# A pair of heads' attention scores made side by side on the two halves of TensorE's rows

## What is computed

```
# per block of 128 queries, 8 heads of 64, 2 heads of keys and values, k_top = 256
logits = einsum('bqhd,bsd->bqhs', q_idx, k_idx) * 64 ** -0.5
score = einsum('bqhs,bqh->bqs', relu(logits), w_idx) * 8 ** -0.5
_, sel = top_k(where(causal, score, -inf), k_top)
s = einsum('bqhgd,bqkhd->bqhgk', q, k[sel]) * 64 ** -0.5      # masked where not valid
o = einsum('bqhgk,bqkhd->bqhgd', softmax(s), v[sel])
```

## Time and profile before

| | us |
|---|---|
| median of 3 runs | 3080.78 |
| the three runs | 3079.59 to 3089.05 |
| span of the profiled execution | 3082.3 |
| PE busy in it | 2955.2 |
| DVE busy | 2238.4 |
| ACT busy | 1631.1 |
| selection stage, from the profile | about 2232 to 2897 |

### The profile page before, as it was taken

One profiled execution on the slowest core, in us unless ns is written; L12 is line 12 of the kernel. 1 busy time (PEld: TensorE's weight loads), 2 busy tenths in 40 slices (PEclk: granted clock), 3 DMA queues, 4 the chain that ended last, 5 costly groups with the idle time before them and its releaser, 6 DMA issues. The chain is left out here.

```text
span 3082.3 us, 48442 instructions
## 1 busy us (share of the span) xinstructions
PE 2955.2 (96%) x17512; PEld 2368.1 (77%) x17512; DVE 2238.4 (73%) x3267; ACT 1631.1 (53%) x2923; POOL 297.2 (10%) x683
## 2 busy tenths in 40 slices
PE   6999999999999999999999999999978899999899
PEld 5888888888878886777777888888756667777687
DVE  8888887766576758889879665535278998888553
ACT  5343422232454546777769534222278899988510
POOL 2000000000000001000100000000022333333100
PEclk8999999999999999999999999999978999999999
DMA  4434422257755423111127334232551111111774
GB/s 123 125 106 119 159 73 69 69 184 246 217 172 139 176 99 115 32 29 56 46 68 234 98 118 137 98 124 77 156 117 42 25 37 24 26 39 41 166 223 139
DMA packets 375235, 334.66 MB, mean 109 GB/s; under 512 B 97275, under 2 KB 328187, under 8 KB 368973
## 3 DMA queue, kind: packets, MB, share of 16 engines
q1 hardware_dynamic: 368676, 294.73, 33.4%
q0 software_dynamic: 5600, 36.51, 3.4%
q10 hardware_dynamic: 720, 0.31, 0.0%
HBM read 212.84 MB, written 108.68 MB: 104 GB/s over the span
## 5 line engine op out<-in xcount | busy, mean ns | idle before, releaser
L349 ACT ACTIVATE s_mx_w_hi<-s_mx_raw 128x512 fp32r<-128x512 f32 x224 | 138.5, 628 | 310.1 <-PE p_oa_acc L705 238.2
L705 PE MATMUL p_oa_acc<-s_h_a_hi,s_mx_w_hi 128*128 128x512 f32 x744 | 291.5, 392 | 8.5 <-DVE s_h_a_lo L448 7.1
L705 PE MATMUL p_oa_acc<-s_h_a_lo,s_mx_w_hi 128*128 128x512 f32 x744 | 290.4, 390 | 0.0
L705 PE MATMUL p_oa_acc<-s_h_a_hi,s_mx_w_lo 128*128 128x512 f32 x744 | 290.4, 390 | 0.0
L1821 DVE TENSOR_TENSOR_SCAN s_st_prod<-s_st_soft,s_st_prod 128x512 f32<-128x512 f32 x192 | 234.9, 1269 | 8.3 <-ACT s_st_soft L1748 7.6
L1748 ACT ACTIVATE s_st_soft<-p_st_z 128x512 f32<-128x512 f32 (+3 forms) x320 | 153.4, 533 | 108.5 <-PE p_st_z L1874 107.7
L3565 PE MATMUL p_sa_turn<-s_ident,s_sa_arg 128*128 128x128 f32 x1088 | 164.9, 287 | 42.2 <-ACT s_sa_prob L3163 22.7
L491 DVE TENSOR_TENSOR s_mx_w_lo<-s_mx_raw,s_mx_w_hi 128x512 fp32r<-128x512 f32 x224 | 153.5, 686 | 53.6 <-ACT s_mx_w_hi L349 52.1
L2654 PE MATMUL p_pr_ps<-s_h_hi,s_pr_w_hi 128*128 128x512 f32 (+1 forms) x680 | 183.1, 390 | 1.2 <-DVE s_pr_w_lo L2509 1.0
L2654 PE MATMUL p_pr_ps<-s_h_hi,s_pr_w_lo 128*128 128x512 f32 (+1 forms) x680 | 182.9, 389 | 0.0
L2654 PE MATMUL p_pr_ps<-s_h_lo,s_pr_w_hi 128*128 128x512 f32 (+1 forms) x680 | 182.9, 389 | 0.0
(11 more groups left out here) (465 smaller groups left out, 7366.7 us busy)
## 6 DMA issues: line engine op xcount, KB each, us to landing
s_mx_raw<-in_w_in_a SPq DMA_DIRECT2D x128, 256.0 KB, 3.9
s_pb_ada<-in_w_ada SPq DMA_DIRECT2D x16, 768.0 KB, 6.6
s_pr_raw<-in_w_in SPq DMA_DIRECT2D x21, 512.0 KB, 6.1
s_pr_work<-s_pr_stage SPq DMA_DIRECT2D x38, 256.0 KB, 4.4
d_rot_hi<-s_pr_rot POOLq DMA_DIRECT2D x9, 1024.0 KB, 4.3
d_rot_lo<-s_pr_stage POOLq DMA_DIRECT2D x9, 1024.0 KB, 6.3
d_y_t<-s_mx_y SPq DMA_DIRECT2D x16, 512.0 KB, 5.6
s_oa_y_raw<-d_y_t SPq DMA_DIRECT2D x16, 512.0 KB, 6.7
```

The source lines that it names most:

```text
L705: ins = nc.tensor.matmul(bank, w[:, m, k, :], a[:, m, k, :], start=(k == 0 and n == 0), stop=(k == KH - 1 and n == 2))
```

## The change

Index scores stay as they are (`whole_scores`). Attention scores are made for a pair of heads and one key part at a time. The query tile now has, for each pair, the high part of the even head on partitions 0 to 63 and of the odd head on 64 to 127, and the low parts likewise behind them; this takes four DMAs a block in place of two. A matmul then uses the 64 rows of one head: three products (high·high, high·low, low·high) for each of the two heads, six matmuls in place of four, the two heads' on different rows of the array and into different banks. Both banks must be free before the first of the six. The list of due times alternates the heads within a key part, so that a pair's products stand side by side.

```diff
 def load_queries(sp, to, landed, b, first, rot_hi, rot_lo):
+    if first == ROT_QI:
...
+    pairs = HEADS // 2
+    for part, of in enumerate((rot_hi, rot_lo)):
+        rows = of[first:first + 512, :].rearrange("(c s d) (t n) -> s t d c n", s=2, d=HD, n=P)
+        for side in range(2):
+            sp.dma_start(to[side * HD:side * HD + HD, b % 2, part * pairs:part * pairs + pairs].bitcast(F32), rows[side, ORDER[b]]).then_inc(landed[b % 2], 16)
...
-        ahead = [("attend", qb, 2 * pair + side, m) for side in range(2) for m in range(len(parts(qb)))]
-        timed += [(s - LEAD + (n + 0.5) / len(ahead), p) for n, p in enumerate(ahead)]
+        ahead = [("attend", qb, 2 * pair + side, m) for m in range(len(parts(qb))) for side in range(2)]
+        timed += [(s - LEAD + (n // 2 + 0.5) / (len(ahead) // 2), p) for n, p in enumerate(ahead)]
...
+                    pe.wait_ge(q_in[qb % 2], 64 * (qb // 2 + 1))
...
+            def scores(kind, qb, pair, m):
+                n, width = number[kind, qb, 2 * pair, m], parts(qb)[m][1]
...
+                for side in range(2):
+                    bank_free(n + side)
+                q = (qi_two if kind == "index" else q_two)[:, qb % 2]
+                q_hi, q_lo = q[:, pair], q[:, PAIRS + pair]
+                hi, lo = keys_of(kind, qb, pair, m)
+                for nth, (one, two) in enumerate(((q_hi, hi), (q_hi, lo), (q_lo, hi))):
+                    for side in range(2):
+                        rows = slice(side * HD, side * HD + HD)
+                        ins = nc.tensor.matmul(pr[(n + side) % BANKS][:, 0:width], one[rows], two[rows], start=nth == 0, stop=nth == 2)
+                        if nth == 2:
+                            ins.then_inc(product, 1)
...
-                    scores(kind, qb, h, m)
+                    if kind == "index":
+                        whole_scores(kind, qb, h, m)
+                    elif h % 2 == 0:
+                        scores(kind, qb, h // 2, m)
```

More of the change, by code:

```diff
@@ L3516, in _, with bank_free @@
             pieces_in = {"index": 0, "attend": 0}
[L3518 to L3530, removed]
+            def bank_free(n):
                 if n >= BANKS:
@@ L3536, in scores, with wait_for_operands, keys_of, whole_scores @@
                         pe.wait_ge(masked, masks[b, head, part] + 1)
-                q = (qi_two if kind == "index" else q_two)[:, qb % 2, h, :]
-                kv = h // (HEADS // KV_HEADS)
-                of = slice(at, at + width)
-                hi, lo = (ki_hi[:, of], ki_lo[:, of]) if kind == "index" else (k_hi[:, kv, of], k_lo[:, kv, of])
-                if kind == "attend" and qb == 0:
-                    hi, lo = (space.k_first[:, part, kv] for part in range(2))
+            def wait_for_operands(kind, qb):
+                if kind == "index":
+                    pe.wait_ge(qi_in[qb % 2], 32 * (place_of(qb) // 2 + 1))
+                else:
+                    pe.wait_ge(q_in[qb % 2], 64 * (qb // 2 + 1))
+                if kind == "attend" and qb == 0:
+                    pe.wait_ge(space.k_first_in, 64 * KV_HEADS)
+                while (kind == "index" or qb) and pieces_in[kind] < len(KEY_PIECES[kind]) and KEY_PIECES[kind][pieces_in[kind]][0] < keys(qb):
+                    pe.wait_ge((ki_in if kind == "index" else k_in)[pieces_in[kind]], 64 if kind == "index" else 64 * KV_HEADS)
+                    pieces_in[kind] += 1
+            def keys_of(kind, qb, pair, m):
+                at, width = parts(qb)[m]
+                kv, of = pair // (PAIRS // KV_HEADS), slice(at, at + width)
+                if kind == "index":
+                    return ki_hi[:, of], ki_lo[:, of]
+                return [space.k_first[:, part, kv] for part in range(2)] if qb == 0 else (k_hi[:, kv, of], k_lo[:, kv, of])
+            def whole_scores(kind, qb, h, m):
+                n, width = number[kind, qb, h, m], parts(qb)[m][1]
+                if h == 0 and m == 0:
+                    wait_for_operands(kind, qb)
+                bank_free(n)
+                q = (qi_two if kind == "index" else q_two)[:, qb % 2, h, :]
+                hi, lo = keys_of(kind, qb, h // 2, m)
                 nc.tensor.matmul(pr[n % BANKS][:, 0:width], q, hi, start=True, stop=False)
```

10 lines of the change are left out of this document (7 added, 3 removed).

## The result

The changed kernel takes 3119.41 us (median of four runs, 3116.77 to 3120.85), the kernel before beside it 3081.19 (3079.59 to 3089.05). The ratio is 1.0119, with a 95% interval of 1.0104 to 1.0133: slower by 38 us, where 35 were forecast. The profiled execution has a span of 3118.8 us against 3082.3. Read from the starts of the matmuls, the 36.5 us between them are made up so: 2.3 stand ahead of the selection stage, in phases that did not change; 33.6 in the stage (664.9 to 698.5 us); 1.2 less between its end and the last phase; 2.1 in the last phase; and the rest is rounding and the very end.

What follows compares the result with a forecast made beforehand. PE was taken to set the pace in blocks 6 to 12. Terms 14.3 + 1.7 + 1 for changes of form and 15 + 3 for ACT's rows made 35 us on 3080.8: 3116, range 3083 to 3142.

Steps and rivals of the forecast that it cites:

- What bounds the kernel: Blocks 6 to 12: PE, busy 113 of 120 and 207 of 213 us, sets the pace; additions to its stream add time.
- The price of a change of form: On PE, 280 changes at 0.20 us, 56 against 31.8 saved; blocks 6 to 12 lose 14.3 us.
- ACT's two rows: Both rows raised in one unit empty buffers later for PE: 15 us in blocks 6 to 12, bounds 0 and 38.
- the halves one behind the other: Rival, chance 0.02: the 64-row halves do not run side by side, six steps for four, 75 us on PE, over 3140.
- 2397 to 2504: Stretch where PE and DVE are both full: 1.7 us from changes of form, 3 from ACT's rows.
- Elsewhere: The other 67 changes of form, 13.4 less 6.9 us, lie where PE has idle time: 1 us; ACT has idle time.
- The new wait for two banks at once: On PE's queue before a group: costed at nothing, as DVE has mostly masked the earlier products by then.
- The rest at nothing: Four query DMAs per block instead of two, the two-bank wait and DVE's unchanged work: costed at nothing.
- that only the forms count: Rival, chance 0.15: ACT's second row is absorbed, only changes of form cost, 17 us, 3098 (3090 to 3102).
- that entering is free: Rival, chance 0.14: on PE only the 120 ways out cost 0.20; 3084, within 0.3%.
- that the type and not the rows costs: Rival, chance 0.09: no change of form costs between two products of the same type; 3067, faster.
- The faster rival: Chance 0.09: changes of form between products of one type are free, 19.5 + 3 us gained where PE is full; 3067.

Runs made afterwards that it cites:

- e10_two_stagger: Changed kernel with the odd head's row raised one unit later and the high-query, low-key product left out (two steps, not three): 3082.25 us.
- e11_three_whole: Kernel before with the change's list, odd head's row one unit later, odd heads' low-key product left out (three 128-row products of four): 3070.94 us.
- e5_before_late: Kernel before with every row raised one unit later where the unit that needs it allows: 3071.58 us, ratio 0.9967.
- e6_order_stagger: Kernel before (four 128-row products) with the change's list and the odd head's row raised one unit later: 3077.02 us.
- e1_order: Kernel before with only the change's list of due times, both rows of a pair raised in one unit: 3099.38 us, ratio 1.0063.
- e9_order_late_stagger: Kernel before with the change's list, the even head's row raised one unit later and the odd head's two: 3120.4 us.
- e7_two: Changed kernel with the high-query, low-key product left out (two steps, not three), rows raised as in the change: 3106.3 us.
- e8_late_stagger: Changed kernel with the even head's row raised one unit later and the odd head's two: 3142.16 us.
- e3_last: Changed kernel with the attention group sorted last in its unit, before the weighing: 3134.33 us.

## Why the prediction came true, point by point

**What bounds the kernel.** "PE sets the pace, and what is added to PE's stream is added to the time" does not hold in full, and below a certain length of the stream not at all. 13.7 us more on PE made blocks 6 to 12 9.7 us longer with the rows apart; with them together it was 5.5 us for 8.4 (325.0 to 333.4, the first of these at a granted clock of 0.99). 19.3 us less gave 9.0 in `e10_two_stagger`; 12.4 less, in `e11_three_whole`, gave nothing there. PE at 0.96 of this stretch was not a bound with idle time behind it; DVE's mask, ACT's raise, ACT's emptying and PE's turning form a ring that turns hardly faster than PE does. That PE's gain reappears as its wait for ACT is shown; how much of the ring is DVE's and how much ACT's is not taken apart, but `e5_before_late`, which removed ACT's wait for masks with no work changed, gained 6 us in this stretch.

**The price of a change of form**, 0.20 us, is right to the hundredth, also for the way that no row of before showed. PE's work in blocks 6 to 12 grew by 13.7 us against 14.3, and over the kernel, by the page's first part, from 2955.2 to 2978.9, 23.7 against 24. That the totals meet so closely is in part luck: with one and the same set of products PE's busy time over the kernel is 2948.8 us in `e6_order_stagger`, 2957.7 in `e1_order` and 2965.4 in `e9_order_late_stagger`, as the waits and the clock vary. The Trainium skill says on its page "TensorEngine Tiling (Array Packing)", under "Key Properties", that a change of the tiling mode drains the engine; the trace agrees, with 0.33 and 0.32 between starts in place of 0.23.

**ACT's two rows**, 15 us in blocks 6 to 12. The wait is as described, 23 times in 28 slots, up to 2.5 us. The sum for these blocks, 29.3, stands beside 26 measured. But the split in it is wrong: the list alone gives 20.4, and the changes of form on top of it 5.5. Part of PE's added work falls into time in which it would have waited for ACT. That the two were set down as terms to be added is the flaw in the working; it did little harm since the one was taken too small by 5 and the other too large by 9, and that they nearly cancel is luck. (By its own factors, 1.4 times 28, the upper bound of this term is 39 and not 38, and the halves one behind the other would cost 63 us by their columns and not 75; nothing hangs on either.)

**2397 to 2504**: from the first transpose of block 4 to that of block 6 it is 107.3 to 111.1, 3.8 us against 4.7. Again the sum is near and the split is not: the list alone makes it 0.6 shorter (106.7), where 3 more were forecast for ACT's rows, and the products add 4.4, where 1.7 were. **Elsewhere**: 1 us was taken, and this term was too small. Blocks 0 to 3 are 4.6 us longer. The start of the stage, before block 0's first unit, is 1.6 longer, but that says little, since it is 10.2 to 12.2 us in the kernels here without a 64-row matmul. Blocks 0 to 3 by the busy time, before and then after:

```profile
2242.30:2396.80 154.50, 118.78 (x659) 92.31 (x659) 121.52 (x266) 126.13 (x306) 33.37 (x74) 0.82 0.33 71
...
2246.20:2405.30 159.10, 122.16 (x710) 86.04 (x710) 119.22 (x264) 124.68 (x304) 35.26 (x74) 0.82 0.30 66
```

PE has 3.4 us more work there and 1.2 us more idle time, so the work did not hide in the idle time, as had been assumed. "The new wait for two banks at once" is not shown to be a cost: PE waits 29.6 us for a bank in these blocks (for ACT's relu or DVE's masks), but it had waited 26.3 us before and 26.8 in `e1_order`, which takes one bank at a time. That leaves up to 3 us for it, not taken apart. That the tail would be shorter was not seen either. This and the 2.3 us of unchanged phases nearly cancel.

**The signs.** The group's three steps, the way in, the way out, the late index product, the stretch of over 333 us and waits for emptied buffers of well over 10.3 us are all there. Two signs are not: PE is busy for 0.93 of blocks 6 to 12 (333.4 of 358.5 us), not over 0.95, and the waits are longer but not fewer, 23 and not 20. Both say the same, that PE's stream is less of a bound than the prediction took it for.

**The rest at nothing**: no wait for the queries' four DMAs is among the stage's. **The rivals**: that only the forms count is refuted by `e1_order`; that entering is free, and that the type and not the rows costs, by the steps above; the halves do run side by side. The faster rival was priced at 3067 from a stream 32 us shorter. `e11_three_whole`, which has that stream, has 4 to 6 us for it. Taken from `e1_order` at 3099, even the 14 us of `e7_two` would leave the change slower than before; that sum is an argument, since no run has such a stream with both rows in one unit.

## What to carry to other kernels

Before adding or subtracting an engine's work at full price because it is 97% busy, ask what the next engine of the ring would do with the time: here, in blocks 6 to 12, an added microsecond cost 0.7 (9.7 of 13.7), and over the kernel a removed one gave 0.1 to 0.5 (4 of 32 to 14 of 32). Two or three kernels with shorter streams show whether the stretch has a length of its own, here 334 or 353 us by the arrangement of the rows. Products on halves of the array need long groups: one of three steps saves 0.23 us, and a change of form at each end costs 0.40. And when work is grouped in pairs on one engine, look at what the same list does to the others: a step that took one row per unit takes two, and moving the second by one unit was worth 28 us, and on the kernel before, with all rows, 10.

## What the runs showed of the hardware

The price of a change of form between 128 and 64 rows is the same in both directions: about 0.10 us before the first product of the new form and 0.10 before the second (0.33 and 0.33 in place of 0.23 and 0.23). From products to the weighing, which uses 64 columns, it is less: 0.09 before the first (0.32) and 0.05 before the second (the trace of the kernel before has matmuls of the weighing at 2615.493, 2615.653 and 2615.763, so 0.16 and then 0.11 apart). A change of type within one form, from float32 transposes to the products, costs nothing: the eighth transpose, at 2613.434, the first product at 2613.463 and the second at 2613.778 take 0.34 us together, once 0.11 and once 0.23. Part of the price goes with the clock: at the lower level, in `e8_late_stagger`, a step is 0.43, the start behind a change comes at 0.56 (2709.96 to 2710.52) and the first step is 0.59 (2708.94 to 2709.53), so 0.13 and 0.16 more.

The granted clock turned a wait into more than its length. In the changed kernel 23 waits for emptied buffers, up to 2.5 us and 20.4 in all, left it at 1.00 over blocks 6 to 12. With 31 such waits and 35.5 us in `e3_last` its mean is 0.97; with 28 waits for a row, up to 2.5 us and 37.8 in all, in `e8_late_stagger` it is 0.94, and PE's work 355.9 us for 331.6 of the same instructions.
